# A two-block transformer kernel on one core: the first sums taken in pairs of feature blocks, and the attention of the second half-layer made in pairs of heads

## The reference, cut to what matters

```python
# layer ab
sh, sc, gt = split(silu(c) @ ab_w_mod + ab_b_mod, 3)       # modulation of x; the same with c_ctx for ctx
h = x * (1 + sc) + sh
z = h @ ab_w_in                                             # 10 chunks of 256 columns; 6 and 7 are the values v
ya = pool(a) ...; yb = u * (w_s @ norm(v) + b_s) ...        # pooling and gated spatial unit
x = layer_norm(ALPHA * x + gt * (concat(ya, yb) @ ab_w_out))
# layer cd
z = h @ cd_w_in                                             # f_in, f_gate, cq, ckv, kr, d_gate
q = rms(cq) @ cd_w_q_up                                     # 8 heads of 64 + 32 (rope on the 32)
k, v = rms(ckv) @ cd_w_kv_up                                # 8 heads of 64 and 64; kr (32, rope) shared by all heads
attn = softmax(q k^T / sqrt(96)) v                          # 512 queries, 768 keys
yc = (fft2(f_in).real @ cd_fnet_w) * silu(f_gate);  yd = attn * silu(d_gate)
x = layer_norm(ALPHA * x + gt * (concat(yc, yd) @ cd_w_out))
```

## Time and profile before

| | |
|---|---|
| median of three executions | 2883.76 us (2883.1 to 2891.36) |
| the profiled execution: its own time | 2889.03 us |
| its span in the trace | 2887.2 us |
| TensorE busy | 2763.7 us, 96% of the span |
| VectorE, ScalarE, GpSimd busy | 1162.8, 957.7, 143.7 us |
| mean granted clock of TensorE | 0.971 of full speed |
| DMA | 250.06 MB, mean 87 GB/s |

### The profile page before, as it was taken

One profiled execution on the slowest core, in us unless ns is written; L12 is line 12 of the kernel. 1 busy time (PEld: TensorE's weight loads), 2 busy tenths in 40 slices (PEclk: granted clock), 3 DMA queues, 4 the chain that ended last, 5 costly groups with the idle time before them and its releaser, 6 DMA issues.

```text
span 2887.2 us, 34955 instructions
## 1 busy us (share of the span) xinstructions
PE 2763.7 (96%) x14803; PEld 2211.6 (77%) x14803; DVE 1162.8 (40%) x1735; ACT 957.7 (33%) x1429; POOL 143.7 (5%) x261
## 2 busy tenths in 40 slices
PE   7999999988999999997999999999999997999998
PEld 5887785557888887774788888888887774788887
DVE  3324652556333244446533324333243446533322
ACT  3222333442222234545322223222135445332221
POOL 0040000001000000001100000000001001100000
PEclk9999999999999999997999999999999997999999
DMA  9521231002332232110233222332232110223231
GB/s 304 186 99 36 82 123 44 1 11 86 103 102 90 100 109 58 58 44 30 74 102 102 90 100 102 102 99 92 102 96 69 59 45 30 73 95 99 91 102 73
DMA packets 208049, 250.06 MB, mean 87 GB/s; under 512 B 6400, under 2 KB 187223, under 8 KB 207895
## 3 DMA queue, kind: packets, MB, share of 16 engines
q1 hardware_dynamic: 207894, 247.83, 26.4%
HBM read 245.72 MB, written 2.10 MB: 86 GB/s over the span
## 4 chain that ended last, share of the span: by engine, by line
PE 88%; DVE 5%; ACT 3%; issue 2%; DMA 1%; POOL 1%; SPq 1%; DVEq 0%; POOLq 0%; ACTq 0%
PE psum L781 85%; PE psum L1243 1%; PE psum L1164 1%; PE psum L851 1%; DVE w_lo L1809 0%; ACT w_hi L1403 0%; DMA mod_w<-in_ab_w_mod 0%; DVE spare_lo L1809 0%; SPq L662 0%; DVE h_lo L1818 0%; ACT softplus L1761 0%; POOL stats_first L2412 0%; ACT softplus L1763 0%; DVE X L1881 0%; DVE stats_first L1885 0%
## 5 line engine op out<-in xcount | busy, mean ns | idle before, releaser
L781 PE MATMUL psum<-h_hi,w_hi 128*128 128x512 f32 (+1 forms) x2096 | 784.5, 374 | 6.6 <-ACT v_a L1412 4.1
L781 PE MATMUL psum<-h_lo,w_hi 128*128 128x512 f32 (+1 forms) x2096 | 778.7, 372 | 0.0
L781 PE MATMUL psum<-h_hi,w_lo 128*128 128x512 f32 (+1 forms) x2096 | 778.4, 371 | 0.0
L1809 DVE TENSOR_TENSOR w_lo<-raw,w_hi 128x2048 fp32r<-128x2048 f32 (+1 forms) x176 | 400.4, 2277 | 796.5 <-ACT w_hi L1403 796.2
L781 PEld LDWEIGHTS psum<-h_hi,w_hi 128*128 128x128 f32 x2096 | 398.1, 190 | 81.0 <-issue 14.7
L781 PEld LDWEIGHTS psum<-h_hi,w_lo 128*128 128x128 f32 x2096 | 397.6, 190 | 67.8
L781 PEld LDWEIGHTS psum<-h_lo,w_hi 128*128 128x128 f32 x2096 | 397.9, 190 | 65.7 <-issue 0.2
L1403 ACT ACTIVATE w_hi<-raw 128x2048 fp32r<-128x2048 f32 (+1 forms) x176 | 332.7, 1893 | 224.5 <-PE psum L781 217.8
L781 PE MATMUL psum<-w_hi,ff_hi 128*128 128x512 f32 x576 | 224.6, 390 | 0.0
L781 PE MATMUL psum<-w_lo,ff_hi 128*128 128x512 f32 x576 | 224.1, 389 | 0.0
L781 PE MATMUL psum<-w_hi,ff_lo 128*128 128x512 f32 x576 | 224.1, 389 | 0.0
(11 more groups left out here) (287 smaller groups left out, 3240.9 us busy)
## 6 DMA issues: line engine op xcount, KB each, us to landing
raw<-in_ffn_w_gate SPq DMA_DIRECT2D x44, 1024.0 KB, 5.3
raw<-in_ffn_w_up SPq DMA_DIRECT2D x44, 1024.0 KB, 5.3
raw<-in_ffn_w_down SPq DMA_DIRECT2D x44, 1024.0 KB, 4.8
raw<-in_w_in SPq DMA_DIRECT2D x36, 512.0 KB, 5.1
raw<-in_ab_w_in SPq DMA_DIRECT2D x10, 1024.0 KB, 7.7
mod_w<-in_ab_w_mod SPq DMA_DIRECT2D x8, 1024.0 KB, 11.8
raw<-in_w_out SPq DMA_DIRECT2D x8, 1024.0 KB, 4.8
raw<-in_cd_w_in SPq DMA_DIRECT2D x7, 1024.0 KB, 5.4
```

What stands on the lines that cost most here:

```text
L781: return pe.matmul(o, lhsT, rhs, start=start, stop=stop, skip_group_check=True)
L1809: dve.tensor_tensor(lo[:, 0:nk * n], raw[c % 2][:, 0:nk * n], hi[:, 0:nk * n].bitcast(F32), ALU.subtract).then_inc(*w_lo_made.mark(key))
```

## The change

Two places, otherwise the program is the same.

**Start.** x is loaded first, then modulation chunks in the order 0, 4, 1, 5, 2, 6, 3, 7 (chunk p carries the shift, chunk p + 4 the scale, of feature blocks 2p and 2p + 1), with the first two chunks of `ab_w_in` (6, and now 0) behind chunk 4. The four token tiles of x are transposed per feature block. As soon as a pair of feature blocks has shift and scale, `parts_of(p)` adds their share to four accumulating products of chunk 6 and to two of chunk 0. Values' second chunk (7) comes later. The late modulation chunks move back.

**Layer cd.** Keys and queries are made for two heads by one product of 128 output rows; the rope parts of the queries are made in two blocks of four heads before the Fourier products and copied into four `qT` tiles. Values and the first pair's keys and queries stand before the `fnet` products. The four chunks of `cd_w_out` are split by quarters between the steps of the attention. The transposes of the attention's output stand behind the first quarter of `down`. The weights of rope, queries, keys and values are loaded by 24 DMAs where there were five.

```diff
+ROPE_AT, ZERO_AT = (2, 0, 3, 1), (None, 1, 2, 0)
+CD_PIECES = {n: divmod(i, 4) for i, n in enumerate((4, 6, 7, 8, 10, 12, 14, 15, 21, 22, 23, 24, 26, 27, 28, 30))}
+MOD_FIRST = (0, 4, 1, 5, 2, 6, 3, 7)
+AB_STEPS = [("turn", 5), ("made", 0, 0, 0), ("made", 0, 1, 0), ("mod", 8), ("v", 6, 4), ("v", 6, 5), ("end", 6), ("split", 7),
+            ("group", 0, 0, 1), ("group", 0, 1, 1), ("end", 0), ("split", 1), ("sgu_w",), ("mod", 9)]
+for _t in range(6):
+    AB_STEPS += [("v", 7, _t), ("vn", _t), ("mod", 10 + _t)]
+AB_STEPS.append(("end", 7))
...
 # SyncE
-            for n in range(8):
-                sp.dma_start(mod_w[n][:, :, :], mod_chunk("ab_w_mod", n * CW)).then_inc(*mod_landed[n].mark(n))
             for t in range(NT):
                 sp.dma_start(X[:, t, :], A["x"][0, t * P:(t + 1) * P, :]).then_inc(*x_landed[t].mark("all"))
-                if t == 1:
-                    raws_to(0)
-            raws_to(1)
+            for n in MOD_FIRST:
+                sp.dma_start(mod_w[n][:, :, :], mod_chunk("ab_w_mod", n * CW)).then_inc(*mod_landed[n].mark(n))
+                if n == 4:
+                    raws_to(1)
...
+            for i in range(4):
+                if i == 2:
+                    raws_to(CHUNK["cd_in", 0] + 6)
+                for k in range(2):
+                    sp.dma_start(q_turn[:, k, :, ROPE_AT[i], :], q_heads[k][:, i::4, NOPE:QK]).then_inc(*mla_landed.mark("q_rope"))
+                sp.dma_start(rope_c[at, :], A["k_rope_cos"][NOPE:QK, :]).then_inc(*mla_landed.mark("rope"))
+                sp.dma_start(rope_s[at, :], A["k_rope_sin"][NOPE:QK, :]).then_inc(*mla_landed.mark("rope"))
+                sp.dma_start(swap[at, at], A["k_rope_swap"][NOPE:QK, NOPE:QK]).then_inc(*mla_landed.mark("rope"))
...
-            raws_to(CHUNK["cd", 0] + 2)
+            raws_to(CHUNK["cd", 0] + 5)
...
 # TensorE, start
+            def parts_of(p):
+                pe.wait_ge(*h_lo_made["xs", p, 1])
+                for t in range(NT):
+                    for k in (2 * p, 2 * p + 1):
+                        mm3(full(("v", 6, t), CW, v_place(6, t)), tokens(h_hi, k, t * P, P), tokens(h_lo, k, t * P, P), w[0][:, k, :],
+                            w[1][:, k, :], k == t % 2 == 0, k == KT - 1)
+                for j in range(2):
+                    for k in (2 * p, 2 * p + 1):
+                        m = mm3(full(event), w[0][:, k, j * P:(j + 1) * P], w[1][:, k, j * P:(j + 1) * P], main_hi[:, k, :], main_lo[:, k, :],
+                                k == 0, k == KT - 1)
-            for n in range(8):
-                mod_product(n, mod_w[n])
-                if n:
-                    mod_turn(n - 1)
-            mod_turn(7)
+            features(0)
+            first_mods(0)
+            features(1)
+            parts_of(0)
+            first_mods(1)
+            first_mods(2)
+            features(2)
+            parts_of(1)
+            first_mods(3)
+            features(3)
+            parts_of(2)
+            turn("xt", 4, CTX[:, 0, :], (4, 5))
+            parts_of(3)
...
 # TensorE, down and attention
                         m = down_part(s, nk, hi, lo, c, i, i * P, ready, chunks == TAIL and n == 0)
+                        if s == "cd" and i == n == 0:
+                            attn_turns()
...
+            for blk in range(2):
+                for k in range(2):
+                    m = mm(bank(b), q_turn[:, k, blk, :, :].rearrange("p g c -> p (g c)"), cqT[:, k, :], k == 0, k == 1)
...
+            for blk in range(2):
+                rope(("rope", blk), q_rope[:, blk, :])
...
+            def pair_keys(p):
+                for r, (off, n) in enumerate(RANGES):
+                    done(mm(bank(b, n), k_up[:, p * P:(p + 1) * P], ckvT[:, off:off + n], True, True), ("keys", p, r))
+            def pair_queries(p):
+                for k in range(2):
+                    m = mm(bank(b), q_nope[:, k, p * P:(p + 1) * P], cqT[:, k, :], k == 0, k == 1)
+            pair_keys(0)
+            pair_queries(0)
             for c in range(2):
                 w = begin(("fnet", c))
...
-                if n < len(seq) and seq[n][0] + 1 < HEADS and seq[n][1] in beside:
-                    beside[seq[n][1]](seq[n][0] + 1)
+                if n < len(seq) - 8 and n % 8 == 1:
+                    pair_keys(n // 8 + 1)
+                if n < len(seq) - 8 and n % 8 == 3:
+                    pair_queries(n // 8 + 1)
...
 # VectorE (ScalarE the same with the copy of the high part)
+            def split_piece(c, i):
+                at = slice(i * BANK, (i + 1) * BANK)
+                dve.wait_ge(*w_hi_made[key, i])
+                dve.tensor_tensor(lo[:, at], raw[CHUNK[key] % 2][:, at], hi[:, at].bitcast(F32),
+                                  ALU.subtract).then_inc(*w_lo_made.mark(key if i == 3 else (key, i)))
...
+                if n < len(seq) - 8 and n % 8 == 5:
+                    pair_ropes(n // 8 + 1)
+                if n in CD_PIECES:
+                    split_piece(*CD_PIECES[n])
```

More of the change, by code:

```diff
@@ L70 @@
             AB_STEPS.append(("group", _ch, _j, _r))
[L71 to L74 removed]
+            AB_STEPS += [("mod", n) for n in MOD_BEHIND.get((_ch, _j, _r), ())]
             if _ch in (4, 5) and _r == 0:
@@ L409, in build @@
         ctx_parts.close()
+        keys_scope = ExitStack()
+        kT = [sb(keys_scope, "kT", [P, LA]) for _ in range(4)]
+        q_rope = sb(keys_scope, "q_rope", [P, 2, L])
+        keys_scope.close()
         wide = [sb(ctx, "wide", [P, D]) for _ in range(2)]
@@ L923, in tensor_program @@
                     t = step[1]
-                    pe.wait_ge(*(x_landed[t] if t < NT else ctx_landed)["all"])
-                    turn("xt", t, X[:, t, :] if t < NT else CTX[:, t - NT, :])
+                    turn("xt", t, CTX[:, t - NT, :], (near.take(), near.take()))
                 elif kind == "v":
                     _, ch, t = step
-                    if t == 0:
-                        begin(("ab_in", ch))
-                    pe.wait_ge(*h_lo_made["xt", t, 1])
-                    project_tokens(("v", ch, t), weights(("ab_in", ch)), CW, h_hi, h_lo, t, rot)
+                    w = begin(("ab_in", ch)) if t == 0 else weights(("ab_in", ch))
+                    if ch == 6:
+                        pe.wait_ge(*h_lo_made["xt", t, 1])
+                    if t % 2 == 0 or ch == 7:
+                        b = claim(5 if ch == 6 else near.take(), ("v", ch, t + 1 if ch == 6 else t))
+                    bank_of["v", ch, t] = b
+                    for k in range(KT):
+                        m = mm3(bank(b, CW, v_place(ch, t)), tokens(h_hi, k, t * P, P), tokens(h_lo, k, t * P, P), w[0][:, k, :], w[1][:, k, :],
+                                k == 0 and v_place(ch, t) == 0, k == KT - 1)
+                    done(m, ("v", ch, t))
                 elif kind == "mod":
                     m = step[1] - 8
-                    s = m % 3 if m < 14 else 0
+                    s = m % 3 if m < 12 else 0
                     pe.wait_ge(*late_landed[s][m])
-                    late_product(8 + m, late_w[s])
+                    late_product(8 + m, late_w[s], ring)
                 elif kind == "sgu_w":
-                    b = claim(rot.take(), "sgu_w")
+                    b = claim(near.take(), "sgu_w")
                     pe.wait_ge(*sgu_w_landed["all"])
@@ L952, in tensor_program @@
                     end(("ab_in", step[1]))
+                    if step[1] == 7:
+                        ring = rot
             mid = Ring([4, 5, 6, 7])
@@ L1107, in tensor_program @@
                 done(m, ("spec", hd))
+            for t in range(6):
+                b = claim(rot.take(), ("vall", t))
+                done(mm(bank(b), ckvT[:, t * P:(t + 1) * P], v_up[:, :], True, True), ("vall", t))
+            def pair_keys(p):
+                for r, (off, n) in enumerate(RANGES):
+                    b = claim(rot.take(), ("keys", p, r))
+                    done(mm(bank(b, n), k_up[:, p * P:(p + 1) * P], ckvT[:, off:off + n], True, True), ("keys", p, r))
+            def pair_queries(p):
+                b = claim(rot.take(), ("queries", p))
+                for k in range(2):
+                    m = mm(bank(b), q_nope[:, k, p * P:(p + 1) * P], cqT[:, k, :], k == 0, k == 1)
+                done(m, ("queries", p))
+            pair_keys(0)
+            pair_queries(0)
             for c in range(2):
@@ L1591, in over_features @@
                     copy(f_cs[hd % 2][:, t, :], event, full(event, 256), f_cs_made, (hd, t))
+            for blk in range(2):
+                copy(q_rope[:, blk, :], ("qr", blk), full(("qr", blk)), q_made, ("rope", blk))
             over_features(0)
@@ L2149, in rope @@
                 dve.wait_ge(*rope_step["cos", event])
-                dve.tensor_tensor(tile, tile, w[0:QK, :], ALU.add).then_inc(*rope_step.mark(event))
+                dve.tensor_tensor(tile, tile, w[:, :], ALU.add).then_inc(*rope_step.mark(event))
             dve.wait_ge(*kept_dve["kvT", 5])
```

(8 more changed lines are left out.)

412 lines of the change are left out of this document (258 added, 154 removed).

## The result

The changed kernel takes 2851.94 us (median of four, 2850.09 to 2855.41) beside 2887.56 us of the kernel before in the same rounds (2883.1 to 2896.43): ratio 0.9874, 95% interval 0.9846 to 0.9903. That is 36 us less; the forecast was 2843 us, 40.5 less than the profiled execution. The profiled execution is the slowest of the four: 2855.41 us of its own, span 2853.3, 33.9 less than the span before; mean granted clock 0.975 (0.971 before), TensorE busy 2741.3 us (2763.7 before).

A forecast was written before the change was run, and what follows sets the result against it. TensorE was taken to bound the kernel, with DMA and a split bounding the start; 3.5 + 14.4 + 7.2 + 15.4 = 40.5 us off 2883.76 gives 2843 us, range 2834 to 2858.

The forecast's parts named there:

- Part 1: Start: TensorE's lost time falls from 27.6 to 24.1 us by earlier first sums; gain 3.5 us, bounds 8 gained to 3 lost.
- rival 1: Start gives nothing: weights 6 land past 25 or the clock falls between modulation products; 2847 to 2850 us, chance 0.14.
- Part 2: Layer cd: keys, queries and ropes made in pairs or blocks take matmuls off TensorE's line; 14.4 us less.
- Part 3: Before and in the attention: three waits go, clock stays up, quarter splits in the loop cost nothing; together 7.2 us less.
- rival 5: Layer cd: paired keys and queries save nothing because products take longer with 128 output rows; 2858 us, chance 0.03.
- rival 3: Attention goes serial: quarter splits delay the next maximum and exponential, steps take 4.5 instead of 2.99 us; 2891 us, chance 0.03.
- Part 4: Into down: from the transposes' begin to the first layer norm 12.8 us instead of 27.8; gain given as 15.4 us.
- Rival 2: Layer norm behind down keeps the gain through VectorE's tiles or late gain rows, 5 instead of 15.4; 2853 us, chance 0.09.
- The small DMAs: 24 weight loads, issued from 387 until 399, cost nothing before rope at 447; opposing rival, landing late: 2853 us, chance 0.03.

The follow-up runs named there:

- e3: The changed kernel with VectorE's low part of each quarter split made one attention step after ScalarE's high part; 2846.14 us, ratio 0.9857.
- e5: The changed kernel run once more, unaltered, on another chip; 2853.16 us, ratio 0.9872.
- e9: e3 with one added wait: TensorE begins the pooling products only after ScalarE has taken ab_in's last gate group out of its bank; 2842.36 us, ratio 0.9837.
- e1: The kernel before with only the changed start, its own cd part kept; 2887.37 us, ratio 0.9995.
- e6: e3 run once more, unaltered, beside the repeated changed kernel; 2848.14 us, ratio 0.9855.
- e8: The changed kernel with all sixteen quarter pieces moved behind the attention loop on both engines; 2852.71 us, ratio 0.9874.
- e11: e3 with the attention's transposes again ahead of the first products into the residual; 2840.95 us in a single execution.
- e2: The changed kernel with the start of the kernel before, so the cd part alone; 2862.44 us, ratio 0.9915.
- e7: e3 with the start of the kernel before; 2847.76 us, ratio 0.9856.
- e4: The changed kernel with ScalarE's high part of each quarter moved ahead of its copy, right behind the exponential; 2848.79 us, ratio 0.9867.
- e12: e9 run once more, unaltered, in another execution; 2842.93 us, ratio 0.9840.
- e10: e3 with VectorE scaling the first two pooling groups ahead of its low part of ab_out's first weight chunk; 2841.40 us, ratio 0.9841.

## Why the prediction was right, and where it was wrong

The median lies in the range, 9 us above the forecast number. Against the profiled execution, by the sum's own steps:

| step | predicted | changed kernel | without the failed step (e3) |
|---|---|---|---|
| start, at the rope | 3.5 | -0.3 (e5: 3.1) | 3.8 |
| rope to first exponential | part of 21.6 | 3.6 | 3.6 |
| attention | the rest of it | 10.9 | 20.0 |
| last exponential to layer norm | 15.4 | 15.1 | 15.1 |
| behind it | 0 | 4.6 | 2.4 |
| sum | 40.5 | 33.9 | 45.0 |

- **Part 1, the start.** The mechanism held: x, chunks and weights came in the forecast order, the first sums at 26.48 where 27.6 was given, weights 6 at 20.98 (21.9). Between 26 and 250 TensorE waited twice, 1.0 and 0.9 us. At the end of `ab_in` (250.63, before 255.98) it had gained 5.3 us, more than the 3.5. Missing from the step was what the new bank order does at the pooling products: the joined pause, the lower clock behind it (e9).
- **Part 1, from there to the rope.** In the first profile of the changed kernel that lower clock took 3.5 us back (50.74 for the stretch against 47.22), and a slice of 0.83 between 320 and 330, behind a pause of 2.5 us that the kernel before has too, took 2.1 more: 5.3 less 3.5 less 2.1 is the -0.3 of the table. From the norm of ab to the rope it is 143.6 to 143.8 us in all three executions with the old start and four of eleven with the new, and 145.1 to 145.7 in the other seven; why the new start meets the slower case more often is open. At the rope the new start is 2.8 us ahead on average over its eight executions with that pause (the changed kernel, e1, e3 to e6, e8, e11; 0.0 to 4.9) against 447.0, the mean of the three with the old one. In the medians only e2 against the changed kernel shows a gain; e1 against before and e6 against e7 show none. Whether the start is worth anything in the end, with the pause, stays open. By its number rival 1 ("The start gives nothing") came nearer than its 0.14; by its mechanism it did not, since weights 6 were in time and the clock fell 230 us later.
- **Part 2, matmuls taken out,** and the stalls of **Part 3**: 21.6 predicted, 3.6 + 20.0 = 23.6 measured in e3. Pairs of heads cost per product what one head cost: from start to start the keys take 1.29 us (1.38 before), the queries 1.82 (1.80); rival 5 is false. Scores over 128 rows, from the second head on, cost nothing more: 1.56 us for four matmuls, as over 96. (The argument for it was not exact: in the rows that it read, keys take 1.43 us for 1536 columns and rope 0.86 for 1024.)
- **Part 3, the failed step: "Cost nothing; if that cover failed, each step would grow by the excess alone."** It compared busy time per engine with the step, 2.3 + 0.57 < 2.99. That was true and beside the point: VectorE's piece waits for ScalarE's and stands ahead of the next maximum, so the two engines form a ring of 3.87 us with idle time on both. The quarters were also longer than given, 0.69 us on VectorE and 0.63 on ScalarE, not 0.57 and 0.48; e3 shows that this alone cost nothing. Sixteen steps x 0.88 = 14.1; by ScalarE's line exactly sixteen take 3.87 us, and some steps behind them are short (1.72 us three times), so that 9.1 remained (109.45 less 100.35). It is rival 3's mechanism ("the quarter splits stand on VectorE ahead of the next maximum") at a fifth of its price, and the sign named for it, idling in front of the probabilities' transposes, is what the waits showed. The rival was priced as a loop through TensorE's scores of the same item, 4.5 us, which did not occur: scores run a step ahead.
- **Part 4, into `down`,** 15.4 against 15.1: 48 products and the transposes, no wait. Rival 2 is false. But it counted the saving gross. e8 shows that the net worth of moving the splits is what they save behind less what they cost within: 10.0 less 9.1 as the change has them, 10.0 as e3 has them. The other 5 us of the step came without any split in the loop. They were not taken apart: 0.4 of them is the transposes' new place (e11); the order of the splits against the tiles, and not waiting for the attention's end with the spare buffers, are the likely rest.
- **The small DMAs**: issued from 387.11 to 404.83, 18 us and not 12, and no product waited. The rule of the Trainium skill (DMA: Bandwidth & Descriptors, Specifications) was not tested by this: the cover was long enough for either.
- **Behind cd** 4.6 us came by clock, unforeseen: the same 10864 matmul records, at a mean granted clock of 0.973 (from slices of 20 us) and not 0.969. e5 had 1.8 of it.

The sum's error of 6.6 us (40.5 less 33.9) is thus: 9.1 for the quarter pieces, 3.8 for the start in that execution, less 2.0 that parts 2 and 3 gave beyond the forecast, less 4.6 of clock, plus 0.3 in `down`. That the number came out so near is in part luck: 13.2 us that did not come stood against 6.6 that nobody had forecast.

## What to carry to other kernels

A step moved beside others costs nothing only if two sums fit under the bound: the busy time of each engine, and the way around every ring of waits that the step joins. If engine A makes a part and B its remainder, put B's part one iteration behind A's: the same work then cost nothing here, 9.1 us before. And after moving work in time or across banks, read the granted clock at the next pause, not only the pause.

## What the runs showed of the hardware that was not expected

- An added wait made a stretch of the kernel faster. Of eight executions with one pause of 1.89 us around 255 us, six had a lower clock between 250 and 270 (0.78 to 0.97; e4 and e8 had 1.00); of five with pauses of at most 1.03 us there (before, e2, e7, e9, e12), none; the one with 1.79 us (e10), none. That the long pause can bring the clock down is what these counts speak for; e9 and e12 alone, two of two, would be too few. The second pause, 3.1 to 3.5 us, had the lower clock behind it in thirteen of fourteen. What it costs can be read directly: 47 matmuls in the changed kernel, 62 in e9, in the same 10 us, a ratio of 0.76 at a granted clock of 0.78, some 6 us of the lower level (1.2 GHz) and the rest of the full one (2.4). The gain shown is 2.4 to 3.4 us (1.3 against e1) in the stretch that ends at the norm of ab. Beyond that stretch it is not shown: at the rope e9 (442.81) is level with e3 (442.94) and e12 (441.57) is 1.4 ahead, and the medians, 3 to 6 us below e3 and e6, come from another chip, where e11 with the long pause was as fast.
- Of this the Trainium skill (TensorE: Matmul & The Clock Gate, The HAM clock gate) says that the window which the gate's monitor looks at is free-running and isn't reset by a kernel's start. The traces agree as far as they go: with the same instructions ahead and the same pause of 1.89 us, e4 and e8 kept the clock and six executions lost it; and of one kernel, e9 has a slice of 0.83 between 320 and 330 where e12 has 1.00.
- The time behind cd, in stages that no experiment touched, was 2212.8 to 2225.4 us with the places of the slow stretches changing. The time goes with the mean granted clock there: 0.969 to 0.970 in before, e1 and e2 (2222.3 to 2225.4 us), 0.972 or 0.973 in ten others (2217.7 to 2220.5), 0.975 in e11 (2212.8). Why these three are lowest is open. Two medians of this kernel 3 to 5 us apart say little by themselves; the attention's length, repeated to 0.1 us, says more.

The best versions run are e9, e12 and e10: 2841 to 2843 us, ratio 0.984 to the kernel before in the same rounds, where the changed kernel has 0.987, with intervals that overlap a little (0.9827 to 0.9856 for e10, 0.9846 to 0.9903 for the changed kernel). What is shown beyond that overlap is in the traces: 9.1 us in the attention, and the microseconds at the norm of ab. The two edits ahead of ab's layer norm were not tried together.
